# Two-layer MoE decoder: the gate weights of the next stage are loaded and split in the last expert chunks

## What is computed

```python
def hierarchical_moe(hn, ...):
    ...                                   # router: two experts per token, sorted by expert
    a = silu(ragged_dot(xs, w_gate, group_sizes)) * ragged_dot(xs, w_up, group_sizes)
    y = ragged_dot(a, w_down, group_sizes) * sg[:, None]
    return zeros.at[stok].add(y)

def per_layer_embedding(h, p_i, g_ple, w_ple_gate, w_ple_up):
    gate = sigmoid(rmsnorm(h, g_ple) @ w_ple_gate)      # w_ple_gate: 1024 x 1024
    return h + gate * (p_i @ w_ple_up)

# reference(), per layer i
h = h + mixer(h)
h = h + hierarchical_moe(rmsnorm(h, g_ffn[i]), ...)
h = per_layer_embedding(h, p[i], g_ple[i], w_ple_gate[i], w_ple_up[i])
if i == 0:
    k_sh, v_sh = shared_kv(h, g_kv, w_k, w_v, cos, sin)
# after layer 1: rmsnorm(h, g_final)
```

## Time and profile before

| | |
|---|---|
| time, median of 3 runs | 4920.65 us |
| time of the profiled execution | 4923.76 us |
| its span, first to last instruction | 4922.1 us |
| granted PE clock over the span | 0.963 of full speed |
| busy: PE, DVE, ACT, POOL | 92%, 58%, 41%, 33% of the span |
| experts of layer 0 (first transfer to last y store) | about 407 to 1577 us |
| combine | about 1580 to 2497 us |
| experts of layer 1 | about 3326 to 4518 us |
| final stage | about 4521 to 4922 us |
| DMA queues | SP's 1069 MB, POOL's 134 MB |

### The profile page before, as it was taken

How to read it: one execution, slowest core, us unless ns; L and a number is a source line. 1 busy time by engine, 2 the same in 40 slices (tenths; PEclk the granted TensorE clock), 3 DMA queues, 4 the chain that set the end, 5 groups by cost and what they waited for, 6 DMA issues and landing times. The chain is left out here.

```text
span 4922.1 us, 93481 instructions
## 1 busy us (share of the span) xinstructions
PE 4512.7 (92%) x30152; PEld 2853.9 (58%) x30217; DVE 2838.9 (58%) x5624; ACT 2037.2 (41%) x2994; POOL 1628.3 (33%) x1161
## 2 busy tenths in 40 slices
PE   7985999999997699999959999985999999996999
PEld 6953776676665244444425555544766766664444
DVE  5775544444443566566559999864445444443666
ACT  6844343343341433333235655534343443331343
POOL 1104344444342111111024555404444544341332
PEclk9987999999999799999979999998999999998999
DMA  8968889888885888888779999849898989884664
GB/s 241 323 232 271 289 291 285 287 275 273 272 285 175 215 225 221 220 225 226 181 160 223 226 224 225 200 187 289 286 291 275 291 280 288 281 265 160 230 234 167
DMA packets 1262603, 1204.65 MB, mean 245 GB/s; under 512 B 925856, under 2 KB 961696, under 8 KB 1262496
## 3 DMA queue, kind: packets, MB, share of 16 engines
q1 hardware_dynamic: 1216416, 1069.05, 74.0%
q0 software_dynamic: 46080, 134.27, 8.2%
HBM read 742.77 MB, written 274.73 MB: 207 GB/s over the span
## 5 line engine op out<-in xcount | busy, mean ns | idle before, releaser
L837 POOL TENSOR_TENSOR ex_w_lo<-ex_raw,ex_w_hi 128x2048 bf16<-128x2048 f32 x192 | 780.7, 4089 | 1106.1 <-ACT ex_w_hi L896 1106.0
L896 ACT ACTIVATE ex_w_hi<-ex_raw 128x2048 bf16<-128x2048 f32 x384 | 707.0, 1900 | 387.2 <-PE ex_ps_y L112 189.1
L1008 PE MATMUL ex_ps_gate<-ex_xT,ex_w_hi 128*128 128x0 bf16 x2048 | 568.3, 278 | 143.4 <-DMA ex_xT<-ex_xrow 109.3
L1009 PE MATMUL ex_ps_gate<-ex_xT,ex_w_hi 128*128 128x0 bf16 x2048 | 568.1, 278 | 0.0
L1010 PE MATMUL ex_ps_gate<-ex_xT,ex_w_lo 128*128 128x0 bf16 x2048 | 567.7, 277 | 0.0
L1008 PE MATMUL ex_ps_up<-ex_xT,ex_w_hi 128*128 128x0 bf16 x2048 | 558.6, 273 | 0.0
L1009 PE MATMUL ex_ps_up<-ex_xT,ex_w_hi 128*128 128x0 bf16 x2048 | 558.5, 273 | 0.0
L1010 PE MATMUL ex_ps_up<-ex_xT,ex_w_lo 128*128 128x0 bf16 x2048 | 558.4, 273 | 0.0
L988 DVE COPY ex_y<-ex_ps_y 128x512 f32 x324 | 224.0, 691 | 566.4 <-PE ex_ps_y L112 566.4
L972 DVE TENSOR_TENSOR ex_aT<-ex_silu,ex_ps_up 128x384 bf16<-128x384 f32 x256 | 141.7, 553 | 684.3 <-PE ex_ps_up L1010 501.0
L110 PE MATMUL ex_ps_y<-ex_w_hi,ex_aT 128*128 128x512 bf16 x1296 | 492.5, 380 | 6.5 <-DVE ex_aT L976 6.5
(11 more groups left out here) (348 smaller groups left out, 9172.2 us busy)
## 6 DMA issues: line engine op xcount, KB each, us to landing
ex_raw<-in_w_exp_gate SPq DMA_DIRECT2D x128, 1024.0 KB, 9.3
ex_raw<-in_w_exp_up SPq DMA_DIRECT2D x128, 1024.0 KB, 11.5
ex_raw<-in_w_exp_down SPq DMA_DIRECT2D x128, 1024.0 KB, 6.2
y_rows<-ex_y SPq DMA_DIRECT2D x162, 512.0 KB, 2.9
up_rows<-rt_up_out SPq DMA_DIRECT2D x64, 512.0 KB, 2.6
cb_hin<-h_mid SPq DMA_DIRECT2D x64, 512.0 KB, 3.7
cb_up_in<-up_rows SPq DMA_DIRECT2D x64, 512.0 KB, 4.5
mix_x<-in_x SPq DMA_DIRECT2D x32, 512.0 KB, 5.1
```

Of the source, the lines that this page charges most:

```text
L837: eng.tensor_tensor(w_lo[u][:, w], raw[:, c, :], w_hi[u][:, w], ALU.subtract).then_inc(lo_done, 1)
L896: act.activation(w_hi[u][:, c * WCHUNK:(c + 1) * WCHUNK], raw[:, c, :], ACT.Copy).then_inc(hi_done, 1)
L1008: pe.matmul(out, hi, x_hi, start=j == 0, stop=False)
L1009: pe.matmul(out, hi, x_lo, start=False, stop=False)
```

## The change

Both layers get an object `GateWeights`, allocated ahead of the expert stage and kept through the stage behind it. It holds the two room tiles that chunks of even number use for their weights (`w_hi[0]`, `w_lo[0]`), the gains, and views: `parts` for the gate weights' halves in the first 8192 columns, `rest` in the last 4096. The loads of w_ple_gate are issued by SP in chunk `2 * full` into the freed landing places 0 to 3, behind the split of the last chunk's part in each, 1 MB each; ACT and DVE convert them in chunk `2 * full + 1` behind slices 1 to 3 (3, 3 and 2 jobs of 128 x 1024). The gain is loaded at the start of the expert stage. In the combine stage `jobs` shrinks to w_q and w_k/w_v, w_k/w_v's halves lie in `rest`, and the places shift: none in `early`; jobs 0 to 3 in step -1, whose loads SP issues behind the turn of tile 0; jobs 4 to 7 loaded ahead of the turn of tile 1, 8 to 15 behind it, all twelve converted in step 0 behind the head. PE's wait for the gate's halves goes. In the final stage everything on the weights goes.

```diff
+def experts_phase(nc, A, C, layer, pre, rot=None):
 
     with ExitStack() as stack:
         m = Mem(nc, f"ex{layer}", stack)
         raw = m.sb("raw", [P, NCHUNK, WCHUNK])
-        w_hi = [m.sb(f"w_hi{u}", [P, NCHUNK * WCHUNK], BF16) for u in (0, 1)]
-        w_lo = [m.sb(f"w_lo{u}", [P, NCHUNK * WCHUNK], BF16) for u in (0, 1)]
+        w_hi = [pre.room[0], m.sb("w_hi1", [P, NCHUNK * WCHUNK], BF16)]
+        w_lo = [pre.room[1], m.sb("w_lo1", [P, NCHUNK * WCHUNK], BF16)]
...
+        PRE = {1: (0, 3), 2: (3, 6), 3: (6, KD)}
...
+                elif follows:
+                    for c in range(KD * D // WCHUNK):
+                        wait_split(sp, q + 1, c)
+                        sp.dma_start(raw[:, c, :].rearrange("p (k n) -> p k n", k=WCHUNK // D), pre.src[c]).then_inc(raw_loaded[c], 16)
...
+            with nc.allow_non_contiguous_dma(reason="one gain per partition, once"):
+                sp.dma_start(pre.g_ple[:], pre.gain).then_inc(gain_loaded, 16)
             e = table(sp, 2, 0, 0, NE - 1)
...
             sp.sem_inc(all_stored, 1)
+            sp.wait_ge(pre_lo, KD)
...
+            def gate_hi(q, f):
+                for k in range(*PRE[f]):
+                    c, half = divmod(k, WCHUNK // D)
+                    act.wait_ge(raw_loaded[c], 16 * (q + 1) + 16)
+                    act.activation(pre.parts[0][:, k, :], raw[:, c, half * D:half * D + D], ACT.Copy,
+                                   scale=pre.g_ple[:, k:k + 1]).then_inc(pre_hi, 1)
+
             def chunk(q, u, follows, refill):
+                first = table(act, 0, q, 0, MAX_TILES)
                 if follows:
-                    first = table(act, 0, q, 0, MAX_TILES)
...
                     act.activation(silu[f % 2][:], ps_gate[f % 2][:, 0:CW], ACT.Silu).then_inc(silu_done, 1)
+                    if not follows and f in PRE:
+                        if f == 1:
+                            act.wait_ge(gain_loaded, 16)
+                            act.wait_ge(down_mm, first * 2 + DOWN_OPEN)
+                        gate_hi(q, f)
...
+                    if not follows and f in PRE:
+                        for k in range(*PRE[f]):
+                            c, half = divmod(k, WCHUNK // D)
+                            dve.wait_ge(pre_hi, k + 1)
+                            dve.scalar_tensor_tensor(out=pre.parts[1][:, k, :], in0=raw[:, c, half * D:half * D + D],
+                                                     scalar=pre.g_ple[:, k:k + 1], in1=pre.parts[0][:, k, :],
+                                                     op0=ALU.mult, op1=ALU.subtract).then_inc(pre_lo, 1)
...
+class GateWeights:
+
+
+    def __init__(self, nc, tag, stack, gate, gain):
+        m = Mem(nc, tag, stack)
+        self.room = [m.sb(n, [P, NCHUNK * WCHUNK], BF16) for n in ("hi", "lo")]
+        self.parts = [r[:, 0:KD * D].rearrange("p (k n) -> p k n", k=KD) for r in self.room]
+        self.rest = [r[:, KD * D:].rearrange("p (k n) -> p k n", k=KD) for r in self.room]
+        self.g_ple = m.sb("g_ple", [P, KD])
+        self.src = gate.rearrange("(c k p) n -> c p k n", p=P, k=WCHUNK // D)
+        self.gain = gain.rearrange("(k p) -> p k", p=P)
+
...
+def combine_phase(nc, A, C, layer, pre, rot):
...
-        wg = m.sb("wg", [P, 2, KD, D], BF16)
-        g_ple = m.sb("g_ple", [P, KD])
-        wq = m.sb("wq", [P, 2, KD, D], BF16)
-        wkv = m.sb("wkv", [P, 2, KD, 2 * KVW], BF16)
+        wq_both = m.sb("wq", [P, 2, KD, D], BF16)
+        wg, wq, wkv = pre.parts, [wq_both[:, h, :, :] for h in (0, 1)], pre.rest
...
-        jobs = [([(A["w_ple_gate"][layer], 0, D)], k, g_ple, wg) for k in range(KD)]
-        jobs += [([(A["w_q"][0], 0, D)], k, g_q, wq) for k in range(KD)]
+        jobs = [([(A["w_q"][0], 0, D)], k, g_q, wq) for k in range(KD)]
         jobs += [([(A["w_k"], 0, KVW), (A["w_v"], KVW, 2 * KVW)], k, g_kv, wkv) for k in range(KD)]
-        GQ = KD + KD
+        GQ = KD
...
-                for vec, gain in ((A["g_ple"][layer], g_ple), (A["g_mix"][1], g_q), (A["g_kv"], g_kv)):
+                for vec, gain in ((A["g_mix"][1], g_q), (A["g_kv"], g_kv)):
...
                     t = s + 1
-                    if isinstance(s, int) and s < 1:
-                        weights(*((0, 8) if s < 0 else (8, 12)))
+                    if isinstance(s, int) and s == 0:
+                        weights(RAW, 2 * RAW)
                     sp.wait_ge(xl_done, t + 1)
...
                     turn(xT[v], x, x_turned)
+                    if isinstance(s, int) and s == -1:
+                        weights(0, RAW)
                     if isinstance(s, int) and s == 0:
-                        weights(12, len(jobs))
+                        weights(2 * RAW, len(jobs))
...
                 act.wait_ge(gain_done, 1)
-                weights(0, 4)
...
                 if isinstance(s, int) and s < 1 and head:
-                    weights(*((4, 8) if s < 0 else (8, len(jobs))))
+                    weights(*((0, RAW) if s < 0 else (RAW, len(jobs))))
...
             def early():
-                dve.wait_ge(gain_loaded, 48)
+                dve.wait_ge(gain_loaded, 32)
                 dve.tensor_scalar(g_q[:], g_q[:], HEAD ** -0.5, None, ALU.mult).then_inc(gain_done, 1)
                 dve.wait_ge(gain_done, 1)
-                weights(0, 4)
...
                     pe.wait_ge(x_turned, 16 * s + 16)
-                    if isinstance(s, int) and s == 0:
-                        pe.wait_ge(w_lo_done, KD)
                     gate(0)
                     gate(1)
...
-        def steps(eng, step, weights):
-
-            for s in (-4, -3):
-                step(s, s % RING)
-            weights(0, KD // 2)
-            step(-2, 2)
-            weights(KD // 2, KD)
-            for s in range(-1, RING):
+        def steps(eng, step):
+
+            for s in range(-4, RING):
                 step(s, s % RING)
...
-                if isinstance(s, int) and s == -4:
-                    for k in range(KD):
-                        sp.dma_start(raw[k][:], A["w_ple_gate"][layer][k * P:(k + 1) * P, :]).then_inc(w_loaded[k], 16)
...
-            with nc.allow_non_contiguous_dma(reason="one gain per partition, once"):
-                sp.dma_start(g_ple[:], A["g_ple"][layer].rearrange("(k p) -> p k", p=P)).then_inc(gain_loaded, 16)
-            steps(sp, step, weights)
+            steps(sp, step)
...
     rot = Rotary(nc)
     route_phase(nc, A, C, 0)
-    experts_phase(nc, A, C, 0, rot)
-    combine_phase(nc, A, C, 0, rot)
+    with ExitStack() as stack:
+        pre = GateWeights(nc, "pre0", stack, A["w_ple_gate"][0], A["g_ple"][0])
+        experts_phase(nc, A, C, 0, pre, rot)
+        combine_phase(nc, A, C, 0, pre, rot)
+
+
+def last_experts(nc, A, C, out):
+
+    with ExitStack() as stack:
+        pre = GateWeights(nc, "pre1", stack, A["w_ple_gate"][1], A["g_ple"][1])
+        experts_phase(nc, A, C, 1, pre)
+        final_phase(nc, A, C, 1, pre, out)
 
```

More of the change, by code:

```diff
@@ L778, in _ @@
             link(dve.tensor_tensor(C.chunks[:, 3, 0:P - 1], C.chunks[:, 0, 1:P], C.chunks[:, 0, 0:P - 1], ALU.subtract))
-def experts_phase(nc, A, C, layer, rot=None):
+def experts_phase(nc, A, C, layer, pre, rot=None):
     with ExitStack() as stack:
@@ L803, in experts_phase @@
             "gate_mm up_mm silu_done a_mul a_done down_mm y_done y_stored")
+        gain_loaded, pre_hi, pre_lo = m.sems("gain_loaded pre_hi pre_lo")
+        PRE = {1: (0, 3), 2: (3, 6), 3: (6, KD)}
         halves = "l e (h k p) n -> (l e h) p k n"
@@ L1328, in weights @@
                     act.wait_ge(w_loaded[n % RAW], landed[n])
-                    act.activation(w[:, 0, k, :], raw[n % RAW][:, 0:sources[-1][2]], ACT.Copy,
+                    act.activation(w[0][:, k, :], raw[n % RAW][:, 0:sources[-1][2]], ACT.Copy,
                                    scale=1.0 if gain is None else gain[:, k:k + 1]).then_inc(w_hi_done, 1)
@@ L1381, in weights @@
                     dve.wait_ge(w_hi_done, n + 1)
-                    dve.scalar_tensor_tensor(out=w[:, 1, k, :], in0=raw[n % RAW][:, 0:sources[-1][2]],
-                                             scalar=1.0 if gain is None else gain[:, k:k + 1], in1=w[:, 0, k, :],
+                    dve.scalar_tensor_tensor(out=w[1][:, k, :], in0=raw[n % RAW][:, 0:sources[-1][2]],
+                                             scalar=1.0 if gain is None else gain[:, k:k + 1], in1=w[0][:, k, :],
                                              op0=ALU.mult, op1=ALU.subtract).then_inc(w_lo_done, 1)
             def early():
-                dve.wait_ge(gain_loaded, 48)
+                dve.wait_ge(gain_loaded, 32)
                 dve.tensor_scalar(g_q[:], g_q[:], HEAD ** -0.5, None, ALU.mult).then_inc(gain_done, 1)
                 dve.wait_ge(gain_done, 1)
-                weights(0, 4)
             def rotate(t, at, src, dst, heads, n, mm, mm_count, pairs):
@@ L1489, in product @@
                 for k in range(kk):
[L1490 removed]
```

(39 more changed lines are left out.)

2 lines of the change are left out of this document (removed).

## The result

The changed kernel takes 4873.6 us (median of 4 runs, 4864.3 to 4878.1), the kernel before 4919.0 beside it; the ratio is 0.990, 95% interval 0.988 to 0.993, so about 45 us were won where 18 were forecast. The profiled execution has a span of 4871.8 us, 50.3 less than before.

The account below looks back on a forecast made before the run. PE bounds inside expert chunks and stands still behind the last while the next stage slowly builds its first tile. Terms: -10.4 - 11.1 + 1.6 + 1.0 + 0.6 = -18.3 us, giving 4902 us, range 4890 to 4914.

Parts of the forecast that it names:

- Slower tiles: Rival: moved addresses slow PE's reads in each of 64 tiles of the two stages behind the experts; +7.3, 4928 us, chance 0.04.
- Combine start -10.4: Layer 0, start of the combine stage: without the eight gate splits the first tanh comes 10.4 us earlier; bounds -5 and -14.
- last chunk +1.6: Last expert chunk, where the gate splits go: slice 3's down product 1.6 us late in layer 0, 0 in layer 1.
- The added wait: Layer 0's combine stage: tile 1's work stands behind the moved w_q loads and splits, eating most of the 13.6 us won.
- (3): Layer 0's combine chain: four w_q loads behind tile 0's turn land from 1607.8 to 1611.8, copied and split by 1614.3.
- Final start -11.1: Layer 1, start of the final stage: all eight splits and loads go, first gate product 11.1 us earlier; bounds -9 and -15.
- Loads in the chunk before: Chunk before the last: four 1 MB gate loads delay nothing, 0 us; the last chunk's turn up to 3 late in layer 0.
- The gain load and the barriers: Gain load ahead of the experts' first weights, +1.0 us; one more closing barrier per layer, +0.6 us.
- Gathers land at once: Rival: without gate loads the first gathers land 3.6 us sooner in layer 0, 3.9 in layer 1; -25.8, 4895 us, chance 0.16.
- Given back: Rival: the combine stage's tile loop, paced by transfers, loses layer 0's 10.4 us; -7.9, 4913 us, chance 0.17.
- the first rival's 0.16: Chance of the rival Gathers land at once, with first gathers landing sooner in both stages: -25.8 us, 4895 us.
- the forecast's 0.63: Chance given to the forecast itself, the steps' sum of -18.3 us over both layers, 4902 us.

Follow-up runs that it names:

- w_q first: Changed kernel with w_q's first four loads in layer 0's combine stage issued ahead of SP's wait for the first tile's `x`, not behind its turn: 4861.6 us (0.989).
- layer 1 alone: Layer 1's experts and final stage as changed, layer 0's as in the kernel before, `xrow` off a multiple of 256: 4907.1 us (0.998).
- Their sum without the address: Changed kernel with one unused 32-byte tile ahead of the experts' `token`, putting `xrow` off a multiple of 256 again: 4904.6 us, 0.998 to the kernel before.
- layer 0's part: Layer 0's experts and combine stage as changed, layer 1's as in the kernel before, `xrow` off a multiple of 256: 4915.0 us (0.9994).

## Why the prediction was wrong

Single traces scatter by some 3 us in a stage, so I took stage lengths from all 17, between DVE's gated rows and the rows of ACT's tanhs in the timelines:

| us | without | with |
|---|---|---|
| experts layer 0, `xrow` off 256 / on 256 | 1099.4 to 1106.5 (10 traces) | 1085.1 to 1090.3 (7) |
| experts layer 1, the same | 1115.5 to 1122.5 (10) | 1102.6 to 1105.8 (7) |
| layer 0, last gated rows to ninth tanh, change off / on | 207.7 to 210.2 (8) | 196.4 to 199.4 (5) |
| the same, w_q first | | 187.0 to 190.8 (4) |
| layer 1, last gated rows to ninth tanh, change off / on | 102.4 to 103.2 (9) | 92.2 to 94.8 (8) |
| ninth tanh to layer 1's first gated rows, change off / on | 1601.7 to 1610.4 (8) | 1602.4 to 1612.5 (9) |

- **The step that failed: the inside of the expert stages, with no term but the last chunk.** The means of the first two lines differ by 15.5 and 15.0 us, and the timed runs give 26 to 31: the term that the sum held at 0 was about -30 us, larger than the whole forecast. The prediction saw that "everything allocated behind moves", but asked only what PE's reads would make of it, in the stages behind, and called it the rival *Slower tiles*, on the other side. It gave no price to a transfer's source. The earlier trace rows has such turns, 4.65 us for two, taken as they stood.
- **Combine start -10.4 and last chunk +1.6: held in the traces.** The means of the third line differ by 11.3; DVE's last gated rows are themselves 1.5 late, so 9.8 net, where the two steps gave 8.8. First row sum at 10.9 (10.1 forecast), ACT's wait 11.1 (10), PE's wait for the tanh 19.5 (20), and 1.5 us at the last slice (1.6).
- **The added wait was priced right and could have been avoided.** (3) put 10 us of waiting on the path; w_q's loads first gives 9 in the table and 12 to 13 in timed runs.
- **Final start -11.1: somewhat large.** The fifth line gives 9.5; layer 1 alone, timed, 9. Most of the miss is the last gather of the first tile: the prediction took 1.1 us off its 9.1, and it landed 9.2 after its issue all the same. DVE waits for tile 1 no longer, but for tile 2: the row sum at 4508.61 has 8.2 us of idle ahead, the gather that the prediction named as late next.
- **Loads in the chunk before: held**, PE doesn't wait longer at either last chunk. The gain load and the barriers (+1.6 in all) are below the scatter.
- ***Gathers land at once*: no**, by those 9.2 us. ***Given back*: not in the combine stage**, whose eight rows of tanhs took 103.6 before and after. Behind it the last line gives back 2 at the mean, within its scatter.
- **Their sum without the address.** Forecast 18.3, with bounds of 13 and 23; 16.3 in the spans of the one pair of traces; timed 10 (5 to 14) for both and 9 and 3 for the parts. So the steps' sum was too large when timed, though their traces held. Part of that is the choice of traces: layer 0's part was profiled in the fastest of its eleven runs, 7.7 us below their median, the kernel before in one 4.8 above its own. What else takes the timed gain below the traces', above all in layer 0, stays open; w_q's loads gave more when timed than in the traces, so it isn't that this stage's start counts for less.
- **A slip in the chances.** Half of the first rival's 0.16 and a tenth of the forecast's 0.63 make 0.14, not the 0.16 that stands as the chance of a time below 4896.

## What to carry to other kernels

When a change adds, drops or resizes an on-chip tile, list the addresses of everything behind it, and look at the starts of those that DMA transposes read: a turn's source belongs on a multiple of its row's 256 bytes. It pays where an engine waits for the turns, as PE does in the expert stages; in the combine stage, where they are hidden, it brought nothing. An unused tile of 32 bytes in the kernel before brought 26 of the 45 us that the whole change did, and 30 and 31 where `xrow` alone moved. And when work goes from the head of a stage, move the loads of what is left up into its place.

## What was not expected of the hardware

- A transpose of 128 x 2048 bf16 values lands sooner when its source begins at a multiple of 256 bytes: 3.6 us from issue at the least and 3.8 to 3.9 at the median, against 4.2 to 4.3 and 4.4 to 4.5. The least duration of SP's instruction is 1315 ns in either case, so it doesn't show this; its median does, 1680 to 1699 against 2066 to 2173. The destination's start didn't matter.
- In the combine stage the medians from issue to landing fell by 0.6 us for `x3` (2048 values a partition, 4.3 to 3.7), 0.3 for `k_row` (1024, 3.7 to 3.4), and 0.1 for `ph` (512, 2.4 to 2.3), each measured once; the durations of the last two (1202 ns both, 1802 and 1827) show nothing.
- Gathers, in rows of 4 KB, didn't clearly land sooner at a multiple of 256: medians of 7.3 to 7.7 us into `xrow` against 7.5 to 7.6 off it, and 7.2 into `y` in both.
- PE's granted clock fell to 0.66 in the 5 us behind one idle of 2.00 us, and stayed at full behind others of 2.04, 2.23 and 3.06.
